# A modulation pair moved into the norm between two layers, and an output matrix split in quarters inside the attention units

## The chip, the cores and the metric

One core of a Trainium2 chip runs the whole program. The metric is the device time of one execution in microseconds (us), as the median of several runs. TensorE (PE) does the matrix products, VectorE (DVE) and ScalarE (ACT) the elementwise work, SyncE (SP) issues the weight loads, GpSimd (POOL) a few small ones.

## What is computed

Two blocks follow each other, on 256 latent and 256 context tokens of width 1024. The first has two hybrid layers, the second an attention layer with a dense feed-forward and a Fourier layer with a mixture of experts. Every norm is scaled and shifted, and every branch is gated, by a modulation that comes from a vector of conditions:

```python
shift, scale, gate = jnp.split(jax.nn.silu(c) @ w_mod + b_mod, 3, axis=-1)      # first block, one matrix a layer
h = rms_norm(x, norm_w) * (1.0 + scale[:, None, :]) + shift[:, None, :]
...
x_new = x + gate[:, None, :] * (y @ w_out)

mod_l = (silu_c @ ada_w[i] + ada_b[i])[:, None, :]                              # second block
sh1_l, sc1_l, g1_l, sh2_l, sc2_l, g2_l = jnp.split(mod_l, 6, axis=-1)
y_l, y_c = diff_attention(h_l, h_c, cos, sin, w_qkv, lq1, lk1, lq2, lk2, subln_g, w_o, lam_init, not last)
x = x + g1_l * y_l
```

In the differential attention each of 8 heads has two softmaxes whose difference is applied to the values. The heads are normed and multiplied by `w_o`, a 1024x1024 matrix.

## The kernel before, in words

**Modulation.** Each third or sixth of a modulation matrix (1024 x 1024) is a "pair" (m, part). Here m is 0 or 1 for the two layers of the first block, 2 or 3 for the second. A pair comes as two chunks of [128 x 8 x 512], 2 MB each. In `mod_half` (L877) eight products multiply one chunk by the few condition columns, four 32-column groups of the array at a time. `mod_pair("mod second")` turns the result back with four small products (L904). The work needs little but PE time and DMA, so it is put between other work. `FILL[l]` (L90) lists the pairs that go between the units of attention l. `NORM_FILL[i]` (L91) lists the pairs that go into norm i: the first half ahead of the norm's sums (`norm_sums`, L916), the second half between the sums and the spreading of the roots (`spread_roots`, L943), and the turn after it. Norm 1, between the two hybrid layers, has none. Norms 2 to 6 have one each.

**Weights.** SP issues all chunks in the order that `weight_chunks` (L180) returns, through a ring of slots of 16 KB a partition. While the first three attention layers' matrices are read, three slots rotate (the fourth holds high parts), so a chunk waits until the chunk three places before it is used. From the differential attention on all four slots serve. Each chunk then takes the slot that is used up first, by `use_rank` (L224). SP waits for `weights_used` of the slot (L733) and then issues (L745). Everything goes through SP in this one order, so a chunk that waits holds back those behind it. Matrices other than modulation are split into a high and a low part: ACT copies the high part (`split1`, L1714, instruction L1723), DVE subtracts it (`low1`, L2257, instruction L2260), 2048 elements a partition at a time.

**The end of a hybrid layer.** The output matrix has four halves of eight 128x512 products three times over. DVE's `residual` (L2235) adds each tile to X. ACT squares it for the next norm (L1658), DVE sums the squares (L2146), and ACT also splits the next weights at k = 0, 2, 4 (`next_halves`). The one at k = 4 of norm 1 is the first half of the next layer's `in.conv`.

**The differential attention** has 16 units, written out as a list of steps in `diff_steps` (L536) that PE, ACT and DVE each walk through. Step s holds scores of unit s, one "row" of the modulation fill (`mod_rows`: four products, half a chunk, eight records in the trace), transposes of unit s-2 (L1300), exponentials of unit s (ACT L1918), scaling of unit s-1 (DVE L2551) and values of unit s-3. `FILL[2]` has five pairs, so 20 rows, `ROWS2`. 16 lie in the units, rows 16 and 17 behind the second tile of the output product, rows 18 and 19 behind the fourth. All rows add up in one PSUM bank that is held meanwhile. ACT copies it out after row 19 (L1914), PE turns it (`mod turn`, L1331) behind everything else, and DVE adds the biases (L2580) before its `residual`. At the values of units 10 and 11 (`WO_AT`) ACT splits half a `wo0` (2048 elements) and DVE takes the low part. The two halves of `wo1` come later. After 12 heads are normed (`mean_heads`, `scale_heads`) and transposed ("heads", L1315), four tiles of the output product are begun on 12 units' heads, head pair 3 is transposed, and `finish` ends the tiles. Then follow four more tiles from `wo1`.

**Norm 4** begins with the residual of the eight tiles on DVE. ACT splits the first half of `w1.0`, the first feed-forward matrix, ahead of the square of tile 6 (`norm(4, x, lambda k: ff_split(0) if k == KT - 2 ...)`), and DVE takes its low part ahead of tile 7 (`before=lambda k: ff_low(0) if k == KT - 1`). Chunk `w1.0` goes into the slot that `wo0` leaves.

The lines that set the order:

```python
FILL = [[(0, 2), (1, 0), (1, 1)], [(1, 2), (2, 0), (2, 1)], [(2, 4), (2, 5), (3, 0), (3, 1), (3, 2)]]
NORM_FILL = {2: [(2, 2)], 3: [(2, 3)], 4: [(3, 3)], 5: [(3, 4)], 6: [(3, 5)]}
...
        WO_AT = (10, 11)
        ROWS2 = 4 * len(FILL[2])
```

Of the kernel before, what the change touches and what calls it, by code (L numbers as in the profile page):

```python
# [31 lines left out]
F32 = mybir.dt.float32  # L32
# [3 lines left out]
ALU = mybir.AluOpType  # L36
# [3 lines left out]
P = 128  # L40
# [42 lines left out]
T_ID, T_SEL, T_PART, T_RED, T_EPS, T_ROW, T_LIMIT, T_FRONT = 0, 128, 136, 137, 142, 143, 145, 160  # L83
T_ONES, T_ROT, T_ROT32 = 160, 288, 416
T_COS, T_SIN, T_COS32, T_SIN32 = 448, 704, 960, 1216
T_DFT, T_DFTC, T_DFTS, T_IOTA, T_UPPER, T_GATHER, T_ALL = 1472, 1728, 2240, 2752, 3040, 3168, 3188


FIRST = [(0, 0), (0, 1)]
FILL = [[(0, 2), (1, 0), (1, 1)], [(1, 2), (2, 0), (2, 1)], [(2, 4), (2, 5), (3, 0), (3, 1), (3, 2)]]  # L90
NORM_FILL = {2: [(2, 2)], 3: [(2, 3)], 4: [(3, 3)], 5: [(3, 4)], 6: [(3, 5)]}  # L91


def constant_table():
# [85 lines left out]
def weight_chunks(a):  # L180

    def cols(w, c0, c1):
        return [(w[:, c0:c1].rearrange("(k p) n -> p k n", p=P), c1 - c0, 0)]

    def mods(parts):
        out = []
        for m, part in parts:
            w = (a["w_mod"][0], a["w_mod"][1], a["ada_w_2"][0], a["ada_w_2"][1])[m]
            out += [(f"mod{m}.{c}", cols(w, 512 * c, 512 * c + 512)) for c in (2 * part, 2 * part + 1)]
        return out  # L190

    def layer(l):
        w = a["w_in"][l]
        small = [(a["mla_w_uq"][l].rearrange("(k p) n -> p k n", p=P), UQ_COLS, 0),
                 (a["mla_w_ukv"][l].rearrange("(k p) n -> p k n", p=P), UKV_COLS, 2 * UQ_COLS)]
        inner = [("in.conv", cols(w, C_CONV, C_GATE)), ("in.q", cols(w, C_Q, C_GK)), ("in.kv", cols(w, C_GK, C_GQ)),
                 ("in.gq", cols(w, C_GQ, C_CONV)), ("in.g0", cols(w, C_GATE, C_GATE + 512)),
                 ("in.g1", cols(w, C_GATE + 512, C_END)), ("pw", cols(a["conv_pw_w"][l], 0, CONV_CH)), ("small", small)]
        return inner, [(f"out{c}", cols(a["w_out"][l], 512 * c, 512 * c + 512)) for c in range(2)]

    inner0, out0 = layer(0)
    inner1, out1 = layer(1)
    qkv = [(f"qkv{c}", cols(a["attn_w_qkv_2"][0], 512 * c, 512 * c + 512)) for c in range(6)]
    wo = [(f"wo{c}", cols(a["attn_w_o_2"][0], 512 * c, 512 * c + 512)) for c in range(2)]
    ff = []
    for c in range(FF_CHUNKS):
        ff.append((f"w1.{c}", cols(a["ff_w1_2"][0], 512 * c, 512 * c + 512)))
        ff.append((f"w3.{c}", cols(a["ff_w3_2"][0], 512 * c, 512 * c + 512)))
    ff += [(f"w2.{m}", cols(a["ff_w2_2"][0], P * m, P * m + P)) for m in range(KT)]
    fo = [(f"fo{c}", cols(a["fnet_w_o_2"][0], 512 * c, 512 * c + 512)) for c in range(2)]  # L210
    return (mods(FIRST) + inner0 + mods(FILL[0]) + out0 + inner1 + mods(FILL[1]) + out1
            + mods(NORM_FILL[2]) + mods(NORM_FILL[3]) + qkv + mods(FILL[2][:4]) + wo + mods(FILL[2][4:])
            + mods(NORM_FILL[4]) + ff
            + fo[:1] + mods(NORM_FILL[5]) + fo[1:] + mods(NORM_FILL[6]))


def build(nc, a, table, out, dumps=None):
# [26 lines left out]
    with ExitStack() as ctx:  # L244
# [83 lines left out]
        HHI2 = view(17000, KT, TOK, memory=scratch_r)  # L328
        OT2 = view(17000, 2 * DA_HEADS, P)
        HEADS_AHEAD = 12  # L330
        WO_AT = (10, 11)
        ROWS2 = 4 * len(FILL[2])
        COND2 = view(16384, KT, ROWS2 + 32)
        DA_SUMS = root[:, 0, 0:4 * DA_HEADS].rearrange("p (i u) -> p i u", i=2)
# [121 lines left out]
        conv_sq = sem("conv_sq")  # L456
        conv_act = sem("conv_act")
        lam_in = sem("lam_in")
        heads_mean = sem("heads_mean")
        heads_seed = sem("heads_seed")  # L460
        silu_ready = sem("silu_ready")
# [74 lines left out]
        def diff_steps():  # L536

            units = 2 * DA_HEADS
            for s in range(units + 3):
                if s < units:  # L540
                    yield "scores", s
                    yield "rows", s
                if 2 <= s < units + 2:
                    yield "transposes", s - 2
                if s < units:
                    yield "exps", s
                if 1 <= s <= units:
                    yield "scale", s - 1
                if s >= 3:
                    yield "values", s - 3  # L550
                if s == units + 1:
                    for g in range(HEADS_AHEAD // 4):
                        yield "heads", g
            rest = iter(range(units, ROWS2))
            for i in range(4):
                if i == 3:
                    yield "heads", 3
                yield "tile", i
                if i % 2:
                    for r in (next(rest), next(rest)):  # L560
                        yield "rows", r
            yield "finish", None
            yield "mod turn", None

        def unit1(l, u):

# [158 lines left out]
        def _(sp):  # L725
# [3 lines left out]
            for i, (_, parts) in enumerate(chunks):  # L729
                s = slots[i]  # L730
                if earlier[i]:

                    sp.wait_ge(weights_used[s], earlier[i])  # L733
                if s == FRONT_RING and earlier[i] == 1:

                    sp.wait_ge(hi_used, WO1)
                if i == len(FIRST) * 2 + 1:

                    sp.dma_start(tab[:, T_FRONT:T_ALL], table[:, T_FRONT:T_ALL]).then_inc(table_rest_landed, 16)
                    for dst, src in late_loads:  # L740
                        sp.dma_start(dst, src).then_inc(late_landed, 16)
                for src, width, off in parts:
                    k = src.shape[1]
                    dst = ring[:, s * SLOT + off:s * SLOT + off + k * width].rearrange("p (k n) -> p k n", k=k)
                    sp.dma_start(dst, src).then_inc(weights_landed[s], 16)  # L745
# [79 lines left out]
        def _(pe):  # L825
# [51 lines left out]
            def mod_half(mp, half):  # L877
# [3 lines left out]
                    row_turn[mp] = (t.g % 8, t.g // 8)  # L881
                    start()
                b = row_turn[mp][0]
                s, w = chunk(f"mod{m}.{2 * part + half}")
                for r in range(2):
                    for q in range(4):
                        last = product(bank[b][32 * q:32 * q + 32, :],
# [1 line left out]
                                       w[:, 2 * q + r, :], half == 0 and r == 0, half == 1 and r == 1)  # L889
                if half:  # L890
                    last.then_inc(bank_ready[b], 1)
                release.append(weights_used[s])

            def mod_pair(what, mp):
                if what == "mod first":
# [130 lines left out]
            def layer1(l):  # L1026
# [137 lines left out]

                counts["mixed"] += (24, 12)[l] + 2
                mixed = counts["mixed"]
                heads = (0, 1, 3, 4, 5, 6, 7, 2)
                for h in range(4):
                    half_columns(f"out{h // 2}",
# [441 lines left out]
        def _(act):  # L1611
# [289 lines left out]
                    split1(QKV1 + 11)  # L1901
            b, n = t.next()
            take(ACT.Exp, lexp[:, :], bank[b][:, 0:2], b, n)
            score_turns, x = {}, []
            for what, u in diff_steps():
                if what == "scores":
# [17 lines left out]
                elif what == "values":  # L1924
# [6 lines left out]
                    if u in (HEADS_AHEAD, 2 * DA_HEADS - 1):  # L1931
# [4 lines left out]
                            .then_inc(heads_seed, 1)  # L1936
                        if batch:
                            split1(WO1 + 2)
                    if u in WO_AT:
                        split1(WO1 + WO_AT.index(u))  # L1940
                elif what == "heads":
                    b, n = t.next()
                    act.wait_ge(bank_ready[b], n + 1)
# [140 lines left out]
        def _(dve):  # L2084
# [438 lines left out]
            def scale_heads(n, u0, u1):  # L2523
# [6 lines left out]
                for u in range(u0, u1):  # L2530
                    v.tensor_scalar(OT2[:, u, :], OT2[:, u, :], ssq[:, 0, u:u + 1], None, ALU.mult)\
                        .then_inc(heads_scaled, 1)

            score_turns, value_turns, tiles = {}, {}, []
            for what, u in diff_steps():
                if what == "scores":
# [17 lines left out]
                    t.skip(1)  # L2554
                elif what == "values":
                    value_turns[u] = t.next()
                    if u in WO_AT:
                        low1(WO1 + WO_AT.index(u))
                    if u == HEADS_AHEAD:
                        mean_heads(0, HEADS_AHEAD, value_turns[HEADS_AHEAD - 1])  # L2560
                    if u == HEADS_AHEAD + 1:
# [286 lines left out]
```

## Time and profile before

| what | value |
| --- | --- |
| median of 3 runs | 1990.99 us (1987.34 to 1991.74) |
| the profiled execution | 1987.53 us |
| its span, first to last instruction | 1985.3 us |
| mean granted TensorE clock | 0.985 |
| busy: PE, DVE, ACT | 97%, 39%, 28% |
| mean DMA rate | 275 GB/s |

Times of the trace count from the start of the span. A row of a timeline gives start, duration, engine, line, operation, result and inputs, partitions and columns, how many records were merged, and in brackets how long the engine was idle before and who released it. f32 products appear as two records each.

### The profile page before, as it was taken

The page shows a single profiled execution, that of the slowest core. Times are in us where ns is not written, and L with a number is a line of the kernel's source. Part 1 is how long each engine was busy: PE and PEld are TensorE (multiplying, and loading weights), DVE is VectorE, ACT ScalarE, POOL GpSimd, SP SyncE. Part 2 cuts the span into 40 slices and gives each one's busy share as a digit, 9 for nine tenths or more (in the row PEclk, how much of TensorE's full clock was granted, in tenths as well). Part 3 has the DMA queues.
Part 4 walks back from the last instruction along what each step waited for, and adds up shares of the span by engine and source line. Part 5 has one row for each costly group of instructions (what it writes and reads, how often), then busy time and mean ns, then how long its engine had stood idle before and what let it go on. Part 6 is the DMA issues. An engine that isn't in the chain of part 4 may idle for free.

```text
span 1985.3 us, 40459 instructions
## 1 busy us (share of the span) xinstructions
PE 1921.0 (97%) x17949; PEld 1180.6 (59%) x17949; DVE 765.2 (39%) x1456; ACT 547.8 (28%) x1006; POOL 31.2 (2%) x48
## 2 busy tenths in 40 slices
PE   5999999999989998999999999999999999999997
PEld 3786467884868746888887353444444353434444
DVE  4853664865673466766556100100101101001003
ACT  4233653445452264655444000010000000000001
POOL 1000000000000000000000000000000000000000
PEclk9989999999989999999999999999999999999999
DMA  9213631326562296555779999999999999999993
GB/s 343 79 48 94 242 110 56 114 87 247 183 241 98 77 353 242 184 207 159 188 240 383 324 413 410 410 414 403 419 399 416 402 414 407 409 410 404 419 397 152
DMA packets 180595, 545.78 MB, mean 275 GB/s; under 512 B 6890, under 2 KB 42369, under 8 KB 163916
## 3 DMA queue, kind: packets, MB, share of 16 engines
q1 hardware_dynamic: 175776, 528.64, 69.9%
q0 software_dynamic: 3888, 12.35, 1.9%
q8 instruction: 144, 2.36, 0.5%
q10 hardware_dynamic: 764, 2.24, 0.3%
q14 instruction: 23, 0.19, 0.0%
HBM read 538.35 MB, written 6.96 MB: 275 GB/s over the span
## 4 chain that ended last, share of the span: by engine, by line
PE 90%; DVE 4%; ACT 2%; DMA 2%; issue 1%; SPq 0%; ACTq 0%; DVEq 0%; PEldq 0%
PE bank L834 86%; PE bank L872 1%; DMA ring<-in_w_mod 1%; DVE ring_r L2260 1%; DMA ring<-in_w_in 1%; PE bank L943 1%; ACT ring_r L1723 1%; DMA ring<-in_ff_w 1%; PE bank L1147 1%; DVE H L2179 1%; DVE H_r L2188 0%; PE bank L1300 0%; DVE scratch L2146 0%; PE bank L1530 0%; ACT scratch_r L1707 0%
## 5 line engine op out<-in xcount | busy, mean ns | idle before, releaser
L834 PE MATMUL bank<-scratch,modrow 128*32 128x384 f32 (+1 forms) x3840 | 355.2, 528 | 1.0 <-PEq L1480 1.0
L834 PE MATMUL bank<-H_r,ring_r 128*128 128x256 f32 (+2 forms) x1296 | 302.3, 315 | 1.4 <-ACT H_r L1634 1.4
L834 PE MATMUL bank<-scratch_r,ring_r 128*128 128x256 f32 (+2 forms) x1280 | 276.4, 342 | 7.8 <-ACT scratch_r L1707 3.7
L834 PEld LDWEIGHTS bank<-scratch,modrow 128*32 128x32 f32 x3840 | 124.9, 110 | 224.1 <-issue 221.8
L834 PE MATMUL bank<-ring,scratch 128*32 128x256 f32 (+2 forms) x4208 | 248.7, 388 | 0.0
L834 PEld LDWEIGHTS bank<-scratch_r,ring_r 128*128 128x128 f32 (+1 forms) x1280 | 214.5, 193 | 38.7 <-ACT ring_r L1723 6.3
L834 PEld LDWEIGHTS bank<-H_r,ring_r 128*128 128x128 f32 (+1 forms) x1296 | 223.6, 189 | 18.5 <-ACT H_r L1634 1.3
L834 PE MATMUL bank<-ring,modrow 128*32 128x512 f32 (+1 forms) x2304 | 232.8, 557 | 0.0
L2751 DVE TENSOR_TENSOR H<-H,bank 128x512 f32<-128x512 f32 (+1 forms) x48 | 29.8, 620 | 443.1 <-PE bank L834 441.2
L834 PEld LDWEIGHTS bank<-ring,scratch 128*32 128x32 f32 (+1 forms) x4208 | 136.4, 110 | 104.8 <-issue 18.5
L834 PE MATMUL bank<-H_r,scratch_r 128*128 128x512 f32 x544 | 192.7, 397 | 0.3 <-DVE H_r L2199 0.2
L834 PE MATMUL bank<-scratch 128*32 128x256 f32 (+5 forms) x2160 | 190.6, 370 | 0.9 <-DVE scratch L2507 0.7
L834 PEld LDWEIGHTS bank<-ring,modrow 128*32 128x32 f32 x2304 | 74.1, 110 | 145.5 <-issue 144.0
L834 PEld LDWEIGHTS bank<-scratch 128*32 128x32 f32 (+4 forms) x2160 | 110.9, 129 | 54.9 <-issue 25.2
L2042 ACT ACTIVATE H<-bank 128x512 f32<-128x512 f32 (+1 forms) x48 | 26.1, 544 | 413.3 <-PE bank L834 413.3
L1629 ACT ACTIVATE scratch<-bank 128x512 f32<-128x512 f32 (+5 forms) x135 | 69.8, 530 | 196.6 <-PE bank L834 144.8
L2273 DVE TENSOR_TENSOR ring_r<-ring,scratch_r 128x2048 fp32r<-128x2048 f32 (+1 forms) x47 | 103.4, 2201 | 43.6 <-ACT scratch_r L1731 42.2
L834 PEld LDWEIGHTS bank<-H_r,scratch_r 128*128 128x128 f32 x544 | 102.6, 189 | 25.4 <-DVE H_r L2199 1.8
L2260 DVE TENSOR_TENSOR ring_r<-ring,ring_r 128x2048 fp32r<-128x2048 f32 (+2 forms) x42 | 92.4, 2201 | 25.6 <-ACT ring_r L1723 24.6
L1731 ACT ACTIVATE scratch_r<-ring 128x2048 fp32r<-128x2048 f32 (+1 forms) x47 | 86.2, 1838 | 42.6 <-PE bank L834 40.6
L1723 ACT ACTIVATE ring_r<-ring 128x2048 fp32r<-128x2048 f32 (+2 forms) x42 | 77.4, 1842 | 62.2 <-PE bank L834 58.9
L2028 ACT ACTIVATE modrow<-bank 128x384 f32<-128x384 f32 x18 | 8.0, 489 | 291.9 <-PE bank L1530 289.3
(262 smaller groups left out, 1621.9 us busy)
## 6 DMA issues: line engine op xcount, KB each, us to landing
ring<-in_moe_w SPq DMA_DIRECT2D x56, 2048.0 KB, 15.2
scratch<-in_moe_w SPq DMA_DIRECT2D x56, 1536.0 KB, 14.3
scratch<-in_moe_w SPq DMA_DIRECT2D x40, 2048.0 KB, 14.7
ring<-in_moe_w SPq DMA_DIRECT2D x40, 1536.0 KB, 13.8
ring<-in_ada_w SPq DMA_DIRECT2D x24, 2048.0 KB, 8.9
ring<-in_ff_w SPq DMA_DIRECT2D x14, 2048.0 KB, 7.7
ring<-in_w_mod SPq DMA_DIRECT2D x12, 2048.0 KB, 13.7
ring<-in_ff_w SPq DMA_DIRECT2D x8, 1792.0 KB, 8.1
```

What stands on the lines that cost most here:

```text
L834: m = nc.tensor.matmul(out_, w, x_, start=first, stop=last)
L872: m = nc.tensor.transpose(dst, src, ident[0:n, 0:n])
L943: last = nc.tensor.matmul(bank[b][m * h:m * h + m, P * tt:P * tt + P], root[:, 3, c:c + 1].broadcast_to([P, m]), ident, start=True, stop=True)
L1147: nc.tensor.matmul(bank[b][64 * i:64 * i + 64, P:2 * P], rinv[:, u % 4, i:i + 1].broadcast_to([P, 64]), ident, start=True, stop=True)
L1629: nc.scalar.activation(dst, src, func, **kw).then_inc(bank_taken[b], 1)
L1723: nc.scalar.activation(high1(n), raw1(n, ring), ACT.Copy).then_inc(hi_ready, 1)
L1731: nc.scalar.activation(ff_high(n), ff_half(n, ring), ACT.Copy).then_inc(hi_ready, 1)
L2042: nc.scalar.activation(SIL[:, r, 0:WIDE[st]], bank[r][:, 0:WIDE[st]], ACT.Silu)\
L2179: last = v.scalar_tensor_tensor(H[:, k, t0:t1], X[:, k, t0:t1], scale_col[:, k, s:s + 1], rs[:, t0:t1], ALU.mult, ALU.mult)
L2260: v.tensor_tensor(raw1(n, ring_r), raw1(n, ring), high1(n).bitcast(F32), ALU.subtract)\
L2273: v.tensor_tensor(ff_half(n, ring_r), ff_half(n, ring), ff_high(n).bitcast(F32), ALU.subtract)\
L2751: v.tensor_tensor(HIDDEN[:, r, 0:WIDE[st]], SIL[:, r, 0:WIDE[st]], bank[3 + r][:, 0:WIDE[st]], ALU.mult).then_inc(mult_done, 1)
```

## The change

Pair (1, 2), the gate of layer 1, leaves the fill of attention 1 and goes into norm 1. Its second chunk does not pass through the ring but lies in scratch (`ASIDE`). It is loaded by SP just ahead of the next layer's `in.conv`, once the attention of layer 0 no longer uses that memory (`aside_free`). All later pairs move up by one: attention 1 has (2, 0), (2, 1), (2, 2), norm 2 has (2, 3), norm 3 has (2, 4), and the differential attention four pairs instead of five. So its rows end with unit 15, and the held bank is copied out there and turned in step 16. `wo0` is loaded two chunks sooner, `wo1` behind the last pair. The first two halves of the output matrix are split in quarters of 1024 elements: ACT at the values of units 8 to 11, DVE at those of units 9 to 12.

```diff
-FILL = [[(0, 2), (1, 0), (1, 1)], [(1, 2), (2, 0), (2, 1)], [(2, 4), (2, 5), (3, 0), (3, 1), (3, 2)]]
-NORM_FILL = {2: [(2, 2)], 3: [(2, 3)], 4: [(3, 3)], 5: [(3, 4)], 6: [(3, 5)]}
+FILL = [[(0, 2), (1, 0), (1, 1)], [(2, 0), (2, 1), (2, 2)], [(2, 5), (3, 0), (3, 1), (3, 2)]]
+NORM_FILL = {1: [(1, 2)], 2: [(2, 3)], 3: [(2, 4)], 4: [(3, 3)], 5: [(3, 4)], 6: [(3, 5)]}
...
-    return (mods(FIRST) + inner0 + mods(FILL[0]) + out0 + inner1 + mods(FILL[1]) + out1
-            + mods(NORM_FILL[2]) + mods(NORM_FILL[3]) + qkv + mods(FILL[2][:4]) + wo + mods(FILL[2][4:])
+    return (mods(FIRST) + inner0 + mods(FILL[0]) + out0 + mods(NORM_FILL[1])[:1] + inner1 + mods(FILL[1]) + out1
+            + mods(NORM_FILL[2]) + mods(NORM_FILL[3]) + qkv + mods(FILL[2][:3]) + wo[:1] + mods(FILL[2][3:]) + wo[1:]
...
-        WO_AT = (10, 11)
+        WO_HIGH_AT, WO_LOW_AT = (8, 9, 10, 11), (9, 10, 11, 12)
+        ASIDE = view(17016, KT, 512)
...
@@ diff_steps
+                if s == units:
+                    yield "mod turn", None
...
-            rest = iter(range(units, ROWS2))
             for i in range(4):
                 if i == 3:
                     yield "heads", 3
                 yield "tile", i
-                if i % 2:
-                    for r in (next(rest), next(rest)):
-                        yield "rows", r
             yield "finish", None
-            yield "mod turn", None
...
@@ SyncE, in the loop over the chunks, behind the wait for the slot
+                if i == index["in.conv"][1]:
+                    sp.wait_ge(aside_free, 1)
+                    sp.dma_start(ASIDE, a["w_mod"][1][:, 512 * 5:512 * 6].rearrange("(k p) n -> p k n", p=P))\
+                        .then_inc(aside_landed, 16)
...
@@ mod_half
-                s, w = chunk(f"mod{m}.{2 * part + half}")
+                aside = (mp, half) == (NORM_FILL[1][0], 1)
+                if aside:
+                    pe.wait_ge(aside_landed, 16)
+                    w = ASIDE
+                else:
+                    s, w = chunk(f"mod{m}.{2 * part + half}")
...
@@ TensorE, layer1, behind the attention
+                if l == 0:
+                    release.append(aside_free)
...
@@ ScalarE
+            def wo_split(quarter):
+                n, rows_ = WO1 + quarter // 2, slice(4 * (quarter % 2), 4 * (quarter % 2) + 4)
...
+                nc.scalar.activation(high1(n)[:, rows_, :], raw1(n, ring)[:, rows_, :], ACT.Copy)\
+                    .then_inc(hi_ready if quarter % 2 else wo_high, 1)
...
-                    if u in WO_AT:
-                        split1(WO1 + WO_AT.index(u))
+                    if u in WO_HIGH_AT:
+                        wo_split(WO_HIGH_AT.index(u))
...
@@ VectorE
+            def wo_low(quarter):
+                n, rows_ = WO1 + quarter // 2, slice(4 * (quarter % 2), 4 * (quarter % 2) + 4)
+                if quarter % 2:
+                    dve.wait_ge(hi_ready, n + 1)
+                else:
+                    dve.wait_ge(wo_high, quarter // 2 + 1)
+                last = v.tensor_tensor(raw1(n, ring_r)[:, rows_, :], raw1(n, ring)[:, rows_, :],
+                                       high1(n)[:, rows_, :].bitcast(F32), ALU.subtract)
...
-                    if u in WO_AT:
-                        low1(WO1 + WO_AT.index(u))
+                    if u in WO_LOW_AT:
+                        wo_low(WO_LOW_AT.index(u))
```

The table loses four columns of `T_GATHER` (20 rows become 16).

## Rows read from the trace of the kernel before

**Rows 1.** The page: shares of the chain of work that ended last.

```profile
PE 90%; DVE 4%; ACT 2%; DMA 2%; issue 1%; SPq 0%; ACTq 0%; DVEq 0%; PEldq 0%
```

**Rows 2.** Timeline, TensorE, differential attention: row 12, transposes of units 13 and 14.

```profile
726.51 1.06 PE L834 MATMUL bank<-ring,scratch 128*32 128x512 f32 x8
...
740.59 1.12 PE L1300 MATMUL bank<-tab,scratch 128*128 128x128 f32 x4 [2.40 <-DVE scratch L2551]
...
747.22 0.95 PE L1300 MATMUL bank<-tab,scratch 128*128 128x128 f32 x4 [3.81 <-DVE scratch L2551]
```

**Rows 3.** The chain of waits, from 725 to 805 us: start, us, what.

```profile
734.10 1.81 ACT scratch_r L1723
...
735.93 2.29 DVE ring_r L2260
...
770.13 10.43 DMA ring<-in_ff_w
```

**Rows 4.** Timeline, steady unit: idle time of ACT and of DVE in it.

```profile
703.46 0.60 ACT L1629 ACTIVATE scratch<-bank 128x512 f32<-128x512 f32 x1 [1.18 <-PE bank L1300]
...
705.40 1.29 DVE L2297 TENSOR_REDUCE nmax<-bank 128x1 f32<-128x512 f32 x2 [1.14 <-PE bank L834]
```

**Rows 5.** Timeline, layer 1: a split of 1024 elements on ACT and on DVE.

```profile
390.71 1.05 ACT L1723 ACTIVATE ring_r<-ring 128x1024 fp32r<-128x1024 f32 x1
391.86 1.23 DVE L2260 TENSOR_TENSOR ring_r<-ring,ring_r 128x1024 fp32r<-128x1024 f32 x1 [1.05 <-ACT ring_r L1723]
```

**Rows 6.** Timeline, from 753 to 771 us: first tile, rows 16 and 17, the turn's additions.

```profile
753.83 0.47 PE L834 MATMUL bank<-H_r,scratch_r 128*128 128x512 f32 x1
...
758.20 1.92 PE L834 MATMUL bank<-ring,scratch 128*32 128x512 f32 x16
...
770.59 0.50 DVE L2580 TENSOR_TENSOR mod<-bank,vec 128x16 f32<-128x16 f32 x5 [2.90 <-PE bank L1331]
```

**Rows 7.** Timeline, from 781 to 792 us: tile 7 on DVE, norm 4 on TensorE.

```profile
781.67 1.92 PE L834 MATMUL bank<-ring,cond 128*32 128x512 f32 x16
...
782.61 2.29 DVE L2273 TENSOR_TENSOR ring_r<-ring,scratch_r 128x2048 fp32r<-128x2048 f32 x1 [2.21 <-ACT scratch_r L1731]
784.82 0.48 DVE L2246 SCALAR_TENSOR_TENSOR X<-bank,mod,X 128x256 f32<-128x256 f32 x1
...
787.40 2.70 PE L834 MATMUL bank<-ring,cond 128*32 128x512 f32 x16
790.03 1.22 PE L943 MATMUL bank<-tab,root 128*128 128x128 f32 x4
```

**Rows 8.** DMA issues of 710 to 711.5, 767 to 768 and 395 to 440 us: median us to landing.

```profile
ring<-in_ada_w SPq DMA_DIRECT2D x1, 2048.0 KB, 14.8
...
ring<-in_ada_w SPq DMA_DIRECT2D x1, 2048.0 KB, 8.0
...
ring<-in_w_mod SPq DMA_DIRECT2D x2, 2048.0 KB, 10.3
```

**Rows 9.** Timeline around norm 1, from 318 to 347 us.

```profile
318.07 0.37 SPq L745 DMA_DIRECT2D ring<-in_w_in  x1
...
328.79 1.92 ACT L1723 ACTIVATE ring_r<-ring 128x2048 fp32r<-128x2048 f32 x1 [7.92 <-PE bank L834]
...
335.76 0.88 DVE L2249 SCALAR_TENSOR_TENSOR X<-bank,mod,X 128x256 f32<-128x256 f32 x2 [1.48 <-PE bank L834]
...
339.44 0.88 DVE L2249 SCALAR_TENSOR_TENSOR X<-bank,mod,X 128x256 f32<-128x256 f32 x2 [2.21 <-issue]
...
341.98 1.05 PE L916 MATMUL bank<-tab,scratch 128*128 128x1 f32 x8 [2.64 <-DVE scratch L2146]
344.05 1.53 PE L943 MATMUL bank<-tab,root 128*128 128x128 f32 x8 [1.01 <-DVE root L2138]
346.78 1.62 PE L834 MATMUL bank<-scratch_r,ring_r 128*128 128x256 f32 x6 [1.20 <-ACT scratch_r L1689]
```

**Rows 10.** Windows in norm 2: us, busy PE, PEld, DVE, ACT, POOL; granted clock, DMA, GB/s.

```profile
552.00:556.00 4.00, 0.64 (x3) 0.64 (x4) 3.05 (x9) 1.26 (x2) 0.00 (x0) 0.61 1.05 387
```

More of the change, by code:

```diff
@@ L85 @@
 T_COS, T_SIN, T_COS32, T_SIN32 = 448, 704, 960, 1216
-T_DFT, T_DFTC, T_DFTS, T_IOTA, T_UPPER, T_GATHER, T_ALL = 1472, 1728, 2240, 2752, 3040, 3168, 3188
+T_DFT, T_DFTC, T_DFTS, T_IOTA, T_UPPER, T_GATHER, T_ALL = 1472, 1728, 2240, 2752, 3040, 3168, 3184
 FIRST = [(0, 0), (0, 1)]
-FILL = [[(0, 2), (1, 0), (1, 1)], [(1, 2), (2, 0), (2, 1)], [(2, 4), (2, 5), (3, 0), (3, 1), (3, 2)]]
-NORM_FILL = {2: [(2, 2)], 3: [(2, 3)], 4: [(3, 3)], 5: [(3, 4)], 6: [(3, 5)]}
+FILL = [[(0, 2), (1, 0), (1, 1)], [(2, 0), (2, 1), (2, 2)], [(2, 5), (3, 0), (3, 1), (3, 2)]]
+NORM_FILL = {1: [(1, 2)], 2: [(2, 3)], 3: [(2, 4)], 4: [(3, 3)], 5: [(3, 4)], 6: [(3, 5)]}
 def constant_table():
@@ L458, in build @@
         lam_in = sem("lam_in")
+        aside_free = sem("aside_free")
+        aside_landed = sem("aside_landed")
+        wo_high = sem("wo_high")
         heads_mean = sem("heads_mean")
@@ L891, in mod_half @@
                     last.then_inc(bank_ready[b], 1)
-                release.append(weights_used[s])
+                if not aside:
+                    release.append(weights_used[s])
             def mod_pair(what, mp):
@@ L1903, in _ @@
             take(ACT.Exp, lexp[:, :], bank[b][:, 0:2], b, n)
+            def wo_split(quarter):
+                n, rows_ = WO1 + quarter // 2, slice(4 * (quarter % 2), 4 * (quarter % 2) + 4)
+                act.wait_ge(weights_landed[slots[index["wo0"][0]]], landed_at[index["wo0"][0]])
+                act.wait_ge(hi_used, WO1)
+                nc.scalar.activation(high1(n)[:, rows_, :], raw1(n, ring)[:, rows_, :], ACT.Copy)\
+                    .then_inc(hi_ready if quarter % 2 else wo_high, 1)
             score_turns, x = {}, []
@@ L2532, in scale_heads @@
                         .then_inc(heads_scaled, 1)
+            def wo_low(quarter):
[6 more added lines that the diff above has]
+                                       high1(n)[:, rows_, :].bitcast(F32), ALU.subtract)
+                if quarter % 2:
+                    last.then_inc(lo_ready, 1)
             score_turns, value_turns, tiles = {}, {}, []
```

## The prediction

> **What bounds the kernel now.** I read the page first: the chain that ended last is 90% TensorE [rows 1]. So only what shortens or fills its idle time, or takes work from it, counts. All the work of the change lies between 318 and 802 us. Behind it the feed-forward and the experts run on TensorE without a pause, so a microsecond gained there arrives at the end as one. Then I read the chain of waits and the timelines where it leaves TensorE.
>
> In the differential attention TensorE waits 2.40 and 3.81 us before the transposes of units 13 and 14 [rows 2]. The chain names the cause: a split of half an output matrix on ACT, then its low part on DVE, 1.8 and 2.3 us, once for each of two halves [rows 3]. They stand in the engines' order ahead of the next unit's maxima and exponentials. In an undisturbed unit ACT is idle for 1.18 us and DVE for 1.14 us [rows 4]. A half fits into neither. After the units TensorE is busy up to the turn of the fill. Then the chain goes through the load of `w1.0`, 10.43 us from issue to landing [rows 3], its split on ACT, its low part on DVE (2.29 us), and only then tile 7 at 784.82 [rows 7], although TensorE had that tile ready at 781.67, where it begins the next work. Norm 1 has a third gap: TensorE waits 2.64 us for the sums and 1.01 us for the roots [rows 9].
>
> **Part 1, quarters.** A split of 1024 elements takes ACT 1.05 us and DVE 1.23 us [rows 5], against 1.18 and 1.14 us free in a unit [rows 4]. ACT fits. DVE lacks 0.09 us a unit, 0.4 us over four, and the transposes have more slack than that, as DVE's low part no longer waits for ACT (one unit lies between). So the two waits of 6.2 us [rows 2] go. New in the same place are ACT's copy of the held bank, the turn on TensorE, and DVE's additions, now ahead of unit 15's scaling. Five additions took 0.50 us [rows 6]. The copy and the turn fall where ACT and TensorE wait anyway, so I charge 0.5: **-5.7 us**. Bounds: -4.2, if copy and turn, about 0.5 us each by their neighbour, the additions, count too. -7.2, since the records after the waits are also stretched by about a microsecond: transposes 1.12 and 0.95 us for work that in step takes less.
>
> Does `wo0` come soon enough? It now goes ahead of the chunks for rows 12 to 15, which each move one place back in the stream. Rows 12 and 13 need the chunk issued at 710.74. That place lands 14.8 us later, at 725.5 [rows 8], and row 12 starts at 726.51 [rows 2]: 1.0 us of slack. DMA is saturated there, so this is the tightest place of the change. I cost it at nothing. If the cover is gone, each microsecond is one of TensorE's.
>
> **Part 2, four rows fewer at the tiles.** Rows 16 to 19 stood as two groups of 16 records, 1.92 us each [rows 6], in a stretch where TensorE had no wait: **-3.8 us**. Behind them heads 3 and its copies on ACT and DVE could now be late. Heads 3 needs the second batch of scaled heads, done some 3 us after the first tile starts at 753.83 [rows 6], and three tiles of an estimated 2.1 us stand before it (four tiles, two groups of rows and heads 3 fill the 16 us up to the turn). The bound is therefore -3.8 to -2.8.
>
> **Part 3, turn and norm 4.** Before, tile 7 came 14.7 us after `w1.0` was issued at 770.13 [rows 3, 7]. Now the last chunk before it, a modulation chunk that was issued between 767 and 768 [rows 8] and shared the DMA with it, is loaded during unit 15. A chunk alone lands in 8.0 us [rows 8]. Then 1.9 us on ACT and 2.3 us on DVE give 12.3 us: **-2.4 us**. TensorE's tile would allow 11.5 (781.67 - 770.13), so the load stays what is late. DVE now begins the residual sooner, as turn and additions no longer stand before it, but that only adds slack to it. Bounds: 0, if it lands in 10.4 us again, and -3.2.
>
> **Part 4, norm 1.** The pair costs TensorE what it cost elsewhere: two halves of 1.92 us and a turn of about 1 us. The first half fits into the 2.64 us of idle time, the turn into the 1.20 us before the first product of `in.conv` [rows 9] together with the shift. The second half stands between the sums, done at 343.03, and the roots at 344.05, where 1.01 us are free [rows 9]: **+0.9 us**. Bounds: +0.3 and +2.8, the latter with the half at twice its time. ACT's copy of the bank (0.6) stands before its first shift of H, which waits for DVE anyway.
>
> The load beside it: SP issues the scratch chunk at 318.07, in the place of `in.q`, and `in.conv` right behind it, where before it had been there long ago. A chunk alone needs 8.0 us, two issued together 10.3 us in the median [rows 8], so the second some 12.6. `in.conv` lands at 331, and ACT wants it at 328.79 [rows 9], ahead of its squares. The lateness of 2.3 us meets 1.48 and 2.21 us of idle time on DVE before tiles 6 and 7 [rows 9]: nothing is left of it at tile 7, 339.44. I take 0, with 1.5 us as upper bound. The Trainium skill, page DMA: Bandwidth & Descriptors, section Queues, rings and completion order, says that on each DMA engine descriptors are consumed in ring order. By that rule the late one is `in.conv`, never the scratch chunk, which speaks against the order that SP has here. With the rule and without it the sum is the same, as the slack covers it.
>
> `in.q` and `in.kv` also come later, but they are split only behind the products of `in.conv`, which begin at 346.78 [rows 9]. The same number of pairs stays in attention 1 and norms 2 and 3, so nothing changes there.
>
> **Sum.** -5.7 - 3.8 - 2.4 + 0.9 = -11.0 us. The profiled execution took 1987.53 us (span 1985.3), so it would take 1976.5. It lies 3.5 us below the median of the runs, 1990.99, to which the same difference is applied: **1980.0 us**. About 0.2% (4 us) is what a measurement can tell from no change.
>
> **Rivals.**
> - *The quarters do not fit* (0.08). ACT has 0.13 us to spare and DVE too little, and both are bound in order to TensorE's events. If each of the five units with a quarter is stretched by some 1.1 us, part 1 gives nothing: -5.3 us, 1985.7. For it: the thin margins. Against: the low part is a unit behind.
> - *The clock holds* (0.22). In norm 4 the half clock makes the second modulation half 2.70 us instead of 1.92 and the roots 1.22 us [rows 7], in norm 1 the roots 1.53 [rows 9], each about twice. With norm 1 filled and the wait in norm 4 cut by 2.4 us, TensorE could stay at 2.4 GHz: another 0.8 + 0.6 + 0.6 = 2.0 us, 1978.0. Against: norm 2 has its fill and is still granted 0.61 [rows 10]. The Trainium skill, page TensorE: Matmul & The Clock Gate, Part 1, says that throttled is the default and activity releases it. By that rule this rival gains, by the row of norm 2 it does not, and I go by the row.
> - *`w1.0` lands no sooner* (0.07). Then part 3 is 0: 1982.4.
> - *The DMA stream falls behind: slower* (0.04). `wo0` now stands ahead of the chunks for rows 12 to 15 in a saturated stream. Past 1.0 us of lateness of the chunk for row 12, TensorE waits in order in each unit. A transfer of 2.1 MB takes 5.4 us at the 387 GB/s of a busy window [rows 10]. The change is slower once these waits exceed 11 us, with three transfers late 16.2 - 1.0 = 15.2 us: 1995.2. Against: the bytes up to that chunk are the same as before, only their names differ.
> - *The load ahead of the use does nothing by itself*: `wo0` issued sooner serves only the quarters. That is in the sum.
>
> **Numbers.** The forecast as it stands has 0.57, the rest 0.02. The range of 8 in 10 takes in the clock rival and the lower bounds (11.0 + 2.0 + 1.5 + about 2 for the scatter of a median: 1974.5) and the quarters that don't fit (1985.7). So 1974.5 to 1986. Faster by over 0.2%: all cases but the last and part of the first rival, 0.9. Within it 0.06, slower 0.04.
>
> **What would show it.** Right: the transposes of units 13 and 14 without a wait, the first tile near 748, two groups of 16 records gone from the tiles, `w1.0` landed in 8 us and tile 7 some 12.3 us after its issue, roots of norm 1 near 345.0. Wrong: a wait of TensorE for a modulation chunk in the units, ACT late at tile 7 of the output product of layer 0, units 11 to 15 longer than the ones before, or a new wait of heads 3 for DVE.

## The result and the profile after

| | before | after |
| --- | --- | --- |
| median of the runs of the comparison | 1990.14 us (1987.34 to 1991.74) | 1977.12 us (1974.65 to 1977.64) |
| the profiled execution | 1987.53 us | 1974.65 us |
| its span | 1985.3 us | 1972.4 us |
| mean granted TensorE clock | 0.985 | 0.987 |

The ratio is 0.992, 95% interval 0.9903 to 0.9937. The change is faster, with 1977.12 us inside the forecast range. The size was forecast too small: 11.0 us, a ratio of 0.9945, just outside the interval. In the profiled executions the difference is 12.9 us. In two of the variants below one execution each fell into a slower state (2211.09 and 2212.68 us, at a granted clock of 0.842 and 0.841), and their medians and ratios leave it out. The shares of the chain are as in [rows 1] within a point.

**Where the time went** is read at places that both traces have, each as the start of a row:

| stretch | before | after | difference | forecast |
| --- | --- | --- | --- | --- |
| start to the last unit's row (unit 15) | 737.12 | 738.72 | +1.60 | +0.9 |
| that row to the first tile | 16.71 | 10.29 | -6.42 | -5.7 |
| first tile to the issue of `w1.0` | 16.30 | 12.20 | -4.10 | -3.8 |
| issue of `w1.0` to tile 7 | 14.69 | 11.88 | -2.81 | -2.4 |
| tile 7 to the first H of norm 4 | 6.47 | 5.19 | -1.28 | 0 |
| first H to the feed-forward | 10.60 | 10.60 | 0 | 0 |

The sum is -13.0 us, and it arrives at the end as the prediction's first part said: from the start of the feed-forward to the end of the span it is 1183.4 us before (from 801.89) and 1183.5 after (from 788.88). That TensorE has no pause there is not quite so (the chain goes over DVE from 1016.60 to 1018.97), but the pauses are the same. Every sign was forecast, but one term was left out (norm 4, from tile 7 to the first H), and four are off by 0.3 to 0.7 us.

The units, timeline of TensorE after, answering to [rows 2]:

```profile
738.72 1.07 PE L839 MATMUL bank<-ring,scratch 128*32 128x512 f32 x8
739.72 0.66 PE L1313 MATMUL bank<-tab,scratch 128*128 128x128 f32 x4
740.72 1.16 PE L839 MATMUL bank<-scratch 128*128 128x128 f32 x8 [0.34 <-ACT modrow L1935]
...
742.15 0.96 PE L1344 MATMUL bank<-tab,modrow 128*128 128x16 f32 x8
...
744.73 0.65 PE L1313 MATMUL bank<-tab,scratch 128*128 128x128 f32 x4 [0.64 <-DVE scratch L2584]
...
746.14 2.22 PE L1328 MATMUL bank<-tab,scratch 128*128 128x128 f32 x12
...
749.01 0.48 PE L839 MATMUL bank<-H_r,scratch_r 128*128 128x512 f32 x1
```

From row to row it is 3.54 us, up to the last one. The waits of 2.40 and 3.81 us are gone. ACT's copy of the bank has left one of 0.34 us, and the scaling one of 0.64 us. The transposes of the first 12 heads take 2.22 us, where they took 1.47 before (751.58 to 753.05): the chain goes there through DVE's scaling of these heads,

```profile
745.20 2.46 DVE scratch L2552 x12
```

so a wait for DVE hides inside that row. The first tile begins at 749.01.

The chain of waits after, answering to [rows 3]:

```profile
761.21 7.62 DMA ring<-in_ff_w
...
768.86 1.93 ACT scratch_r L1744
...
773.09 0.49 DVE X L2267
```

`w1.0` lands in 7.62 us in place of 10.43. Norm 4, timeline of TensorE, answering to [rows 7]:

```profile
772.06 1.92 PE L839 MATMUL bank<-ring,cond 128*32 128x512 f32 x16
775.14 0.61 PE L927 MATMUL bank<-tab,scratch 128*128 128x1 f32 x4 [1.16 <-DVE scratch L2167]
775.67 1.92 PE L839 MATMUL bank<-ring,cond 128*32 128x512 f32 x16
777.53 0.71 PE L954 MATMUL bank<-tab,root 128*128 128x128 f32 x4
```

The half takes 1.92 us in place of 2.70, the roots 0.71 in place of 1.22: the granted clock held. The windows of the kernel before and of the changed one (columns as in [rows 10]) show it, first those before, where TensorE had been idle for 3.27 us ahead of the sums:

```profile
786.00:790.00 4.00, 3.14 (x20) 0.94 (x20) 1.22 (x6) 0.52 (x2) 0.00 (x0) 0.80 1.05 401
790.00:794.00 4.00, 3.77 (x19) 3.46 (x16) 2.52 (x7) 2.01 (x4) 0.00 (x0) 0.50 1.05 389
```

```profile
774.00:778.00 4.00, 2.86 (x24) 1.41 (x24) 1.50 (x7) 1.01 (x3) 0.00 (x0) 1.00 0.94 316
778.00:782.00 4.00, 3.02 (x17) 1.91 (x15) 3.54 (x9) 2.37 (x6) 0.00 (x0) 1.00 1.05 393
782.00:786.00 4.00, 3.82 (x12) 2.69 (x12) 3.11 (x9) 3.17 (x5) 0.00 (x0) 0.57 1.05 387
```

After, the half clock comes only behind 782 us, while DVE's H tiles set the pace. There it costs nothing: from the first H to the feed-forward it is 10.60 us in both kernels.

Norm 1, timelines of the engines after, answering to [rows 9]:

```profile
318.04 0.37 SPq L745 DMA_DIRECT2D scratch<-in_w_mod  x1
...
331.28 1.92 ACT L1736 ACTIVATE ring_r<-ring 128x2048 fp32r<-128x2048 f32 x1 [10.45 <-DMA ring<-in_w_in]
...
341.95 1.05 PE L927 MATMUL bank<-tab,scratch 128*128 128x1 f32 x8 [0.78 <-DVE scratch L2167]
342.94 1.92 PE L839 MATMUL bank<-scratch,cond 128*32 128x512 f32 x16
...
344.79 1.16 PE L954 MATMUL bank<-tab,root 128*128 128x128 f32 x8
345.78 0.98 PE L915 MATMUL bank<-tab,modrow 128*128 128x4 f32 x8
345.99 3.22 DVE L2200 SCALAR_TENSOR_TENSOR H<-X,scale_col,bank 128x256 f32<-128x256 f32 x8 [2.02 <-PE bank L954]
```

`in.conv` is late by 2.5 us for ACT (331.28 against 328.79), and the sums still start where they did, 341.95 against 341.98. The roots come 0.74 us later and take 1.16 us in place of 1.53, so the first H starts at 345.99, against 345.62 before: +0.37 us. Between it and the transposes of layer 1 (400.13 against 398.65) another 1.1 us are lost. Windows before:

```profile
344.00:348.00 4.00, 2.75 (x14) 2.48 (x15) 2.38 (x7) 3.00 (x6) 0.00 (x0) 0.58 0.79 253
348.00:352.00 4.00, 4.00 (x22) 4.00 (x22) 4.00 (x12) 1.43 (x4) 0.00 (x0) 0.56 0.00 0
...
364.00:368.00 4.00, 3.91 (x32) 3.91 (x33) 3.82 (x8) 0.66 (x2) 0.00 (x0) 1.00 0.99 361
```

And after:

```profile
344.00:348.00 4.00, 3.61 (x29) 2.62 (x22) 2.02 (x6) 3.09 (x6) 0.00 (x0) 1.00 1.06 394
348.00:352.00 4.00, 4.00 (x28) 3.49 (x28) 4.00 (x12) 1.81 (x5) 0.00 (x0) 1.00 0.33 110
...
360.00:364.00 4.00, 1.86 (x9) 1.87 (x10) 2.85 (x5) 3.35 (x4) 0.00 (x0) 0.79 0.05 5
364.00:368.00 4.00, 4.00 (x29) 4.00 (x29) 3.82 (x7) 0.23 (x1) 0.00 (x0) 0.79 1.00 335
```

Before, the half clock lay, but for the roots, where DVE's H tiles set the pace (DVE is busy all of 348 to 352), and there it cost nothing: from the first H to DVE's low part ahead of the next products it took 16.13 us before (345.62 to 361.75) and 16.12 after (345.99 to 362.11). After, it is gone there and turns up at 360 to 368 us, behind a wait for ACT, where TensorE's own products set the pace.

### The profile page after: what moved, and what is told of

It is laid out like the page before. It is cut to its first block, busy times and chain, and to the rows that moved or that the text cites. A ratio compares the mean times of both kernels' runs of the same rounds, so it can differ in the third digit from the quotient of the medians.

```text
span 1972.4 us, 40477 instructions
## 1 busy us (share of the span) xinstructions
PE 1917.8 (97%) x17957; PEld 1176.2 (60%) x17957; DVE 765.0 (39%) x1458; ACT 548.4 (28%) x1009; POOL 31.2 (2%) x48
## 4 chain that ended last, share of the span: by engine, by line
PE 90%; DVE 3%; DMA 3%; ACT 2%; issue 1%; SPq 0%; ACTq 0%; DVEq 0%; PEldq 0%
PE bank L839 87%; PE bank L877 1%; DMA ring<-in_w_mod 1%; DMA ring<-in_attn_w_qkv 1%; DMA ring<-in_w_in 1%; ACT ring_r L1736 1%; PE bank L954 1%; PE bank L1158 1%; DVE H L2200 1%; DVE H_r L2209 0%; DVE ring_r L2281 0%; PE bank L1313 0%; DMA ring<-in_ff_w 0%; PE bank L1543 0%; ACT scratch_r L1720 0%
## 5 line engine op out<-in xcount | busy, mean ns | idle before, releaser
L839 PE MATMUL bank<-scratch,modrow 128*32 128x384 f32 (+1 forms) x3840 | 355.2, 528 | 1.0 <-PEq L1493 1.0
```

The lines of the kernel that those rows point to most:

```text
L839: m = nc.tensor.matmul(out_, w, x_, start=first, stop=last)
```

## The experiments

My theory was the one of the sum, with one addition from the trace: the short wait for `w1.0` keeps the clock in norm 4. Rivals: the gain of the units belongs to the earlier load and not to the quarters; the turn's new place or the four rows carry it; the clock in norm 4 follows something else than that wait. Spans of single executions of one kernel scatter by up to 15 us (part of it is in the last section), so single steps are compared by stretches of the trace, and totals by medians.

**Whole halves.** The changed kernel with `wo0` split in whole halves at units 10 and 11 again.

```diff
-                    if u in WO_HIGH_AT:
-                        wo_split(WO_HIGH_AT.index(u))
+                    if u in (10, 11):
+                        split1(WO1 + (10, 11).index(u))
```

and so for the low parts.

> The changed kernel with wo0 split in two whole halves at units 10 and 11 again, all else kept. Theory (the quarters alone take away the waits before the transposes of units 13 and 14, 6.4 us in the changed kernel's trace): both waits are back, the first output tile starts 6 us later than in the changed kernel (749.0), span 1972.4 + 6 = about 1978.4. Rival (the gain of the units comes from the turn or the rows that moved): span within 1.5 us of 1972.4.

Measured: 1987.31 us, ratio 0.997 (0.9956 to 0.9985), by the ratios 10 us over the changed kernel. The last row to the first tile takes 18.91 us against 10.29, so the quarters are worth 8.6 us here, more than the 6.4 by which this stretch fell. Timeline of TensorE:

```profile
740.55 0.66 PE L1313 MATMUL bank<-tab,scratch 128*128 128x128 f32 x4 [2.40 <-DVE scratch L2584]
743.03 2.02 PE L839 MATMUL bank<-scratch 128*128 128x128 f32 x8 [1.83 <-ACT modrow L1935]
747.18 1.11 PE L1313 MATMUL bank<-tab,scratch 128*128 128x128 f32 x4 [2.13 <-DVE scratch L2584]
```

The 6.36 us of waits, 1.83 of them now ahead of the values, are nearly those of [rows 2], and what follows them is stretched: values 2.02 us against 1.16 after, transposes 1.11 against 0.65. The chain there has the turn at 1.52 us. In step it takes 0.81. So behind such waits the turn too is paid in full and at the lower clock.

**The pair in attention 1.** Norm 1 is left empty, and attention 1 has four pairs.

```diff
+FILL = [[(0, 2), (1, 0), (1, 1)], [(1, 2), (2, 0), (2, 1), (2, 2)], [(2, 5), (3, 0), (3, 1), (3, 2)]]
+NORM_FILL = {2: [(2, 3)], 3: [(2, 4)], 4: [(3, 3)], 5: [(3, 4)], 6: [(3, 5)]}
```

> The changed kernel with pair (1, 2) in attention 1 as a fourth pair and norm 1 empty, no load aside. Theory (the pair costs 1.5 us net in norm 1 and layer 1's start, of it 1.1 us by half clock at 363 to 366, and its full TensorE time of 3.84 + 1.0 = 4.8 us in an attention without idle time): the sums of squares of layer 1 (L877, near 400.3) come 1.5 us sooner, the end of attention 1 is 3.3 us later, span about 1975.7. Rival (the half clock falls there with or without the fill): the first gain is only 0.4 us, span about 1976.9.

Measured: 1981.36 us, ratio 0.9955 (0.9933 to 0.9976). From layer 1's transposes to the last row it takes 342.85 us against 338.59: the pair costs 4.3 us where TensorE has no gap (4.8 were expected). In norm 1 and the start of layer 1 it costs, against the kernel before, 1.5 us in the changed kernel's first profile and 0.4 in its second one (below). The norm is a gap that the pair fills. The roots of norm 1, behind the old waits of 2.64 and 1.01 us, are slow again, in the timeline of TensorE:

```profile
343.00 1.87 PE L950 MATMUL bank<-tab,root 128*128 128x128 f32 x8 [1.01 <-DVE root L2153]
```

In the four profiles without the pair in norm 1 (the kernel before, this one and the two with the quarters alone below) the roots took 1.53, 1.87, 2.07 and 2.08 us, in all nine with it 1.16. So it is the fill, with the shorter waits that it leaves, that keeps the clock there.

**`in.conv` ahead of the scratch chunk.** SP's two loads exchanged.

```diff
+                for src, width, off in parts:
+                    ...
+                    sp.dma_start(dst, src).then_inc(weights_landed[s], 16)
                 if i == index["in.conv"][1]:
                     sp.wait_ge(aside_free, 1)
                     sp.dma_start(ASIDE, ...)
```

> The changed kernel with in.conv issued ahead of the scratch chunk. Theory (the late in.conv is covered by slack on VectorE): in.conv lands near 326, ScalarE splits it at 328.8 and no longer at 331.3, and tile 7's residual stays at 339.4, the sums at 341.95: span 1972.4, same within 0.5. Rival (the lateness is on the path): 1 to 2.5 us faster.

Measured: 1978.22 us, ratio 0.9937 (0.9921 to 0.9954). DMA issues around 318 us, of the changed kernel and then of this one:

```profile
scratch<-in_w_mod SPq DMA_DIRECT2D x1, 2048.0 KB, 7.8
ring<-in_w_in SPq DMA_DIRECT2D x1, 2048.0 KB, 12.8
```

```profile
ring<-in_w_in SPq DMA_DIRECT2D x1, 2048.0 KB, 7.9
scratch<-in_w_mod SPq DMA_DIRECT2D x1, 2048.0 KB, 12.8
```

Whichever is issued second lands 12.8 us after its issue, as estimated (12.6). By this the trace agrees with the rule of ring order that the prediction cites from the Trainium skill, page DMA: Bandwidth & Descriptors, section Queues, rings and completion order. ACT's split is back at its old distance, and the time is not less: the slack on DVE had covered it.

**The turn at the end**, behind the last tile as before.

> The changed kernel with the turn of the fill behind the last tile again, the rows still ending with unit 15. Theory (turn and additions stand ahead of unit 15's scaling, and behind the tiles they only meet slack, since tile 7 waits for w1.0): the first output tile comes 0.5 to 0.9 us sooner, tile 7 keeps its 11.9 us from the issue of w1.0, span about 1971.7. Rival (the turn at the end delays the residual as before): tile 7 comes 1 us later from the issue, span 1972.4 to 1973.0.

Measured: 1978.82 us, ratio 0.993 (0.9911 to 0.9949). The last row to the first tile takes 10.17 us against 10.29, the issue of `w1.0` to tile 7 12.5 against 11.9. So the turn in step 16 costs 0.1 us and saves 0.6, which totals can't show. The expectation had it the other way round: 0.5 to 0.9 us to gain ahead of the first tile, nothing to lose behind it. It costs so little as it lies in a wait: without it TensorE waits 0.60 us for ACT's next values instead:

```profile
748.57 1.13 PE L838 MATMUL bank<-scratch 128*128 128x128 f32 x8 [0.60 <-ACT scratch L1641]
```

**Quarters and order without the rest.** The kernel before, with the quarters, `wo0` behind the third pair and `wo1` behind the fourth; and the same with the old order of loads.

```diff
-            + ... + qkv + mods(FILL[2][:4]) + wo + mods(FILL[2][4:])
+            + ... + qkv + mods(FILL[2][:3]) + wo[:1] + mods(FILL[2][3:4]) + wo[1:] + mods(FILL[2][4:])
```

> The kernel before with the quarters alone: wo0 loaded behind the third pair, wo1 behind the fourth, five pairs, turn last, norm 1 empty. Theory (the quarters alone take 6.4 us): from row 15 to the first output tile 10.2 us instead of 16.7, from the tile to the issue of w1.0 16.3 as before, from there to tile 7 14.7 as before; 6.5 us in all, 0.33% faster than the kernel before. Rival (the four fewer rows or the moved turn are needed for it): 14 us or more from row 15 to the tile.

> The same, with wo0 and wo1 loaded in the old order behind four pairs. Theory (wo0 lands 13.1 us after an issue at 717.8, at 730.9, and ScalarE wants it at 726.9): ScalarE waits 4 us for it at unit 8, 2 us of slack before the transposes cover half, so TensorE waits some 2 us once and the gain is 4 to 4.5 us. Rival (the sooner load matters nothing): 6.5 us, no wait of TensorE in the units.

Measured: 1984.15 us, ratio 0.9956 (0.9937 to 0.9976), and 1989.22 us, ratio 0.9974 (0.9955 to 0.9992). From layer 1's transposes to the first tile it is 355.2 us in the kernel before, 349.1 with quarters, 353.1 with quarters in the old order. So 6.1 us belong to both together, and 4.0 of them are lost without the earlier load. The layers ahead of the units scatter in this stretch. From the row of unit 15 to the first tile alone it is 10.03 us in both, against 16.71 before: 6.7 us gained, with neither a copy of the bank nor a turn in between. Waits stand there all the same, in the timeline of TensorE with the quarters:

```profile
743.82 0.65 PE L1301 MATMUL bank<-tab,scratch 128*128 128x128 f32 x4 [0.99 <-DVE scratch L2572]
744.93 1.13 PE L835 MATMUL bank<-scratch 128*128 128x128 f32 x8 [0.46 <-ACT scratch L1630]
```

The changed kernel takes 10.29 us, so copy, turn and additions cost it 0.26 us. The chain of waits of the kernel with the old order names what it lost ahead of unit 15:

```profile
721.04 13.64 DMA ring<-in_attn_w_o
...
734.70 0.05 ACT scratch_r L1910
```

`wo0` lands at 734.68. ACT comes to its first quarter, waits 4.4 us for it, and keeps the exponentials behind it waiting.

**A late `w1.0`.** The changed kernel, with the load of mod3.7 held back until just ahead of it.

```diff
+                if i == index["mod3.7"][0]:
+                    sp.wait_ge(lo_ready, WO1 + 4)
```

> The changed kernel with the second chunk of pair (3, 3) held back until the last low part of the output matrix is done, so that it is issued just ahead of w1.0. Theory (w1.0's landing is what is late in norm 4, and the granted clock there follows TensorE's wait): w1.0 lands 12.6 us after its issue, tile 7 comes 16.8 us after it instead of 11.9, and from tile 7 to the first scaled H it takes 6.5 us again instead of 5.2, as the clock falls to 1.2 GHz: 6.2 us slower than the changed kernel. Rival (the clock is a matter of chance): 4.9 us slower, 5.2 us from tile 7 to H.

Measured: 1985.81 us, ratio 0.9963 (0.9946 to 0.9979). The chain has `w1.0` landing 13.17 us after its issue, tile 7 comes 17.4 us after it (+5.5), and from tile 7 to the first H it takes 7.44 us (777.74 to 785.18) in place of 5.19 (6.5 were expected). Timeline of TensorE, and the windows:

```profile
779.79 1.01 PE L929 MATMUL bank<-tab,scratch 128*128 128x1 f32 x4 [6.80 <-DVE scratch L2169]
780.74 3.64 PE L841 MATMUL bank<-ring,cond 128*32 128x512 f32 x16
```

```profile
774.00:778.00 4.00, 0.00 (x0) 0.00 (x0) 2.47 (x2) 1.74 (x2) 0.00 (x0) 0.97 1.02 390
778.00:782.00 4.00, 2.21 (x12) 1.33 (x16) 2.11 (x8) 0.68 (x2) 0.00 (x0) 0.50 0.42 130
```

Here the load comes later and TensorE waits longer; norm 4 has the same fill and the same products. The half takes 3.64 us at a granted clock of 0.50, that is 1.2 GHz. So the longer wait brings the half clock back, and not the fill decides norm 4's clock. All the profiles agree. In the nine in which the wait ahead of the sums was 0.29 to 1.32 us (the two of the changed kernel among them), the stretch took 5.18 to 5.20 us every time. In the four with 3.27 to 6.80 us the clock fell. Among these it was not one and the same loss. Behind 3.34 us the kernel with the quarters alone has, in the timeline of TensorE,

```profile
782.80 3.64 PE L835 MATMUL bank<-ring,cond 128*32 128x512 f32 x16
```

and the one with the old order 3.64 us as well, behind 3.29, where the kernel before took 2.70 us behind 3.27. From tile 7 to the first H it is 7.82 us in both, against 6.47 before. So what the short wait gives back in norm 4 is 1.3 us against the one profile of the kernel before, and 2.6 us against these two.

**`w1.0` sooner.** It is loaded ahead of mod3.7, into the slot that is free after unit 15, and ACT's split and DVE's low part are taken earlier.

```diff
-            + mods(NORM_FILL[4]) + ff
+            + mods(NORM_FILL[4])[:1] + ff[:1] + mods(NORM_FILL[4])[1:] + ff[1:]
...
+        if name == "w1.0":
+            return i + 1.5
...
-            norm(4, x, lambda k: ff_split(0) if k == KT - 2 else None)
+            norm(4, x, lambda k: ff_split(0) if k == 2 else None)
...
-            ... before=lambda k: ff_low(0) if k == KT - 1 else None ...
+            ... before=lambda k: ff_low(0) if k == KT - 2 else None ...
```

> The changed kernel with w1.0 loaded ahead of the second chunk of pair (3, 3), into the slot free after unit 15, split on ScalarE ahead of the square of tile 2 and taken low on VectorE ahead of tile 6. Theory: w1.0 has landed when the tiles end, tile 7 follows TensorE's own tile, 10.9 us after wo0's slot is free instead of 11.9: 1.0 us faster than the changed kernel. Rival (something else is late there, VectorE's row of residuals): less than 0.3 us.

Measured: 1976.3 us, ratio 0.9912 (0.9887 to 0.9938). The chain of waits no longer goes through DMA:

```profile
757.26 16.02 PE bank L841 x91
...
773.52 0.50 DVE X L2269
```

First tile to tile 7 takes 23.2 us against 24.1: 0.9 us, and TensorE is what is late now.

**All on one chip, five rounds.** The changed kernel unedited, `w1.0` sooner, and that with `in.conv` first.

> The changed kernel unedited, beside its two variants on one chip. By the theory (the wait for w1.0 and the clock that it costs norm 4 are what the change took away, beside the units and the tiles) it stands 11 to 15 us under the kernel before: ratio 0.993. The stage between the last row and the feed-forward network as in its first profile: tile 0 to w1.0's issue 12.2, issue to tile 7 11.9, tile 7 to the first H 5.2 us. The rival that its first run owed something to a lucky feed-forward stage (227.7 us, where three variants showed 232.1) gives a ratio of 0.995.

> w1.0 loaded ahead of mod3.7 and in.conv issued ahead of the scratch chunk, together. Theory (ring order costs norm 1 nothing as VectorE has the slack; w1.0 sooner takes the last 0.9 us of the wait): 0.9 us under the changed kernel, and no more from the load's order, 1975.5 to 1977. Rival (the two stretches of waiting add up, and norm 1 gives another 0.4 us with the half clock displaced): 2 us under the changed kernel.

> w1.0 loaded ahead of mod3.7, timed again beside the changed kernel. Tile 0 to tile 7 23.2 us against 24.1 in the changed kernel, so 0.9 us under it, ratio to the kernel before 0.9925; by the rival that the time is set elsewhere (the half-speed stretches of layer 1 fall as they like, 1.5 us each) no difference that five rounds show.

Measured: unedited 1976.79 us, ratio 0.9932 (0.9914 to 0.9949); `w1.0` sooner and `in.conv` first 1976.95 us, 0.9932 (0.9914 to 0.995); `w1.0` sooner alone 1973.03 us, 0.9914 (0.9894 to 0.9933). The intervals overlap. The version with `w1.0` sooner had the lower median beside the changed kernel, and tile 0 to tile 7 again took 23.2 us, which shows the 0.9 us in the trace; that it is faster in total by that much the medians don't show. `in.conv` first adds nothing.

The unedited kernel's second profile has the stretches of its first: row to tile 10.3, `w1.0`'s issue to tile 7 12.0, then 5.2 us. Only the start of layer 1 differs. Its first 24 products there, first profile and then second, in the timeline of TensorE:

```profile
362.14 4.64 PE L839 MATMUL bank<-scratch_r,ring_r 128*128 128x256 f32 x24 [2.18 <-ACT ring_r L1736]
```

```profile
362.13 2.17 PE L839 MATMUL bank<-scratch_r,ring_r 128*128 128x256 f32 x16 [2.18 <-ACT ring_r L1736]
364.46 1.22 PE L839 MATMUL bank<-scratch_r,ring_r 128*128 128x256 f32 x8 [0.15 <-DVE ring_r L2281]
```

The same wait of 2.18 us stands ahead of both, and in the second the clock did not fall. From the sums of norm 1 to layer 1's transposes it took 57.1 us in the second, 58.2 in the first, 56.7 before. Of the nine profiles with the pair in norm 1, three showed the fall there and six didn't.

## Why the prediction was right or wrong

*What bounds the kernel, and that a microsecond gained ahead of 802 us arrives at the end*: right. -13.0 us at the start of the feed-forward, -12.9 in the span.

*Part 1, the quarters*: right in kind, too small by 0.7 us. The quarters alone gave 6.7 us from the row of unit 15 to the first tile, where the sum had the 6.2 of the waits, and copy, turn and additions cost 0.26, where it had 0.5. The 6.7 are 6.21 us of waits gone, less 0.99 + 0.46 of new ones, so 1.9 us more came from the products: those behind the waits had been stretched (values 1.92 us in the unit of the first wait, 1.16 after), and that outweighs the 0.7 us by which the heads' transposes are longer now. The failed step is that I left this stretch as a bound, at "about a microsecond", and put only the waits into the sum, and that I saw no new wait behind the last row. The two omissions hid each other in part, so that the term came out within 0.7 us is partly luck. The lower bound is also added up wrongly: -5.7 with copy and turn at 0.5 each is -4.7, not -4.2. The need for the earlier load is shown: 4.0 us are lost without it.

*The slack of 1.0 us for row 12*: held, rows stand 3.54 us apart throughout.

*Part 2, the rows*: -4.1 against -3.8. The two groups were read at their durations, 1.92 us each. Heads 3 had no wait.

*Part 3, `w1.0`*: the mechanism held, -2.8 against -2.4. The load took 7.6 us, not the 8.0 of the row used. That the load stays what is late was right too: loaded sooner, another 0.9 us go and TensorE's tile is the bound (the forecast had 12.3 - 11.5 = 0.8).

*Part 4, norm 1*: +0.37 us up to the first H against +0.9, as the roots ran at the full clock: 1.16 us against 1.53. With the half clock at the start of layer 1 another 1.1 us were lost in that execution; in the one that didn't have it, +0.4 is all. The cover for `in.conv`'s lateness was named rightly, and exchanging the loads, where ring order puts the lateness on the scratch chunk, gained nothing.

*The rival of the clock* is where the prediction went wrong. It came true in norm 4, for 1.3 us where I had worked out 0.8 + 0.6 = 1.4, and for the roots of norm 1, for 0.4 us (1.53 to 1.16) where I had 0.6. It had a chance of 0.22 and stood outside the sum. The failed step is the argument that put it aside: "norm 2 has its fill and is still granted 0.61". Norm 2 showed that a fill doesn't keep the clock; the question in norm 4 was the wait ahead of it, which the sum itself shortened by 2.4 us. The page TensorE: Matmul & The Clock Gate of the Trainium skill, Part 1, says that throttled is the default and activity releases it. In norm 4 the trace agrees with it: 1.00 behind 1.16 us of idle time, 0.50 behind 3.34 and 6.80. It doesn't settle the start of layer 1, where behind the same 2.18 us two executions of one kernel differ.

By terms, then, the 2.0 us that the sum lacked are 1.3 of norm 4's clock, 0.7 in the units, 0.3 in the tiles and 0.4 in the load, less 0.7 at norm 1 and the start of layer 1.

## What to carry to other kernels

When a change shortens a wait of TensorE, ask what the products behind that wait cost at the other clock, and put that into the sum. A neighbouring stage with work beside it but another wait says nothing about it. Splitting a side job so that each piece fits into the idle time of one step of the pipeline took away waits and what they stretched, but with the load left where it was 4.0 us of that were lost: the operand has to be there for the first piece. A microsecond of half clock costs only where TensorE sets the pace; where DVE did, it cost nothing.

## What was not expected of the hardware

The feed-forward ran at two speeds at the same granted clock of 1.00. Products there, by form, at 840 to 940 us, of the changed kernel:

```profile
L839 PE MATMUL bank<-H_r,scratch_r 128*128 128x512 f32 x285 | 98.8, 394 | 0.0
```

and of the kernel with `in.conv` first:

```profile
L839 PE MATMUL bank<-H_r,scratch_r 128*128 128x512 f32 x284 | 100.4, 399 | 0.0
```

Those with 256 columns took 277 and 281 ns. From the first H of norm 4 to the group of 224 products that the chain has behind the feed-forward it took 245.0 us in the kernel before, 245.0 in both profiles of the changed one, 245.0 to 245.8 in seven variants, and 249.4 to 250.5 in the other three, none of which touches the feed-forward. These three ran on one chip, but so did a fourth profile with 245.5 us, so the chip alone doesn't explain it. These 4 to 5 us are a large part of the scatter between executions, and the cause is open. The half clock at the start of layer 1, which comes or not behind the same idle time of 2.18 us, is open as well: it was not tried what decides it.
